# One-hots of a gate crossing: made by VectorE in one operation, multiplied by the gates on ScalarE

## The chip, the cores and the metric

The kernel runs on one core of one Trainium2 chip. The metric is the device time of one execution, in microseconds (us). The core has five engines that run their own instruction lists and meet at semaphores: TensorE (PE; PEld is its weight load), VectorE (DVE), ScalarE (ACT), GpSimd (POOL) and SyncE (SP).

## The reference

Three blocks of layers follow each other over 256 tokens of width 1024: two layers of feed-forward and mixed attention, two layers of feed-forward with a convolution and with stick-breaking attention, and a third block of two attention layers, each followed by a "peer" layer. This case is about the peer layers alone. Each of the 8 heads picks 16 of 128 x 128 experts for a token, so 128 (first key, second key, gate) triples a token:

```python
def peer_ffn(x, w_q, sub_keys, u, v):
    q = (x @ w_q).reshape(B, S, PEER_HEADS, 2, hq)
    s_half = jnp.einsum('bshpc,hpkc->bshpk', q, sub_keys).astype(jnp.float32)
    top_s, top_i = lax.top_k(s_half, PEER_TOPK)
    ...
    gate = jax.nn.softmax(best_s, axis=-1)
    def one_chunk(args):
        xc, ec, gc = args
        h = jax.nn.gelu(jnp.einsum('ted,td->te', u[ec], xc))
        return jnp.einsum('te,ted->td', gc.astype(h.dtype) * h, v[ec])
```

## The kernel before

The kernel gathers no expert. It computes the hidden values of all 16384 experts for all tokens, multiplies them by a dense matrix of gates that is zero where an expert was not picked, and sends all through the second matrix. Weights come in slabs of 1 MB (128 x 2048 floats). SyncE loads them into a ring of 4 (`RING`), ScalarE rounds each into a high part (`round_slab`, L1388, ring of `PARTS` = 3), VectorE subtracts to get the low part (`rest_slab`, L1867), and TensorE multiplies three products for every pair of tiles (L630, L631, L632).

A peer stage has 64 rounds of "up" (two key rows a round, one slab) and 64 of "down". The first 32 rounds of up run while VectorE picks the experts. Then the **crossing** begins, which this change is about: 14 further rounds of up (`EXTRA`), cut into 28 half rounds, with 32 batches of 8 tokens between them (`v.batches`: none in the first two half rounds and none in the last two, and one or two after each of the 24 between, so 2.67 a round). For a batch b:

- VectorE makes `firsts` (L2515, one operation over 8 x 128) and `seconds` (L2518, eight operations, one a token: compare the second key with 0..127 and multiply by the gate in the same instruction). Both have two buffers, so batch b waits until batch b - 2 is crossed.
- TensorE's `cross` (L1367) multiplies, for each token, firsts by seconds: the 128 x 128 matrix of gates of that token, in PSUM.
- VectorE's `multiply` (L2533) applies one half of the gates to hidden values that lie in SBUF. ScalarE's `stage_gates` (L1794) then copies the other half out of PSUM, and `store_gates` (L1801) sends it to DRAM one batch later; it comes back in the second half of the stage.

Each engine's list is in the order of the code. In a round, ScalarE has `round_slab`, then the batches of its first half round, then `activate` (the Gelu of the up round, L1828), then the batches of its second half round. VectorE has `rest_slab`, then the batches. After the crossing, `separate` (L1837 on ScalarE, L2547 on VectorE) makes the hidden values ready for the first round of down on TensorE. ScalarE stood before `separate` in this order: store of the last batch, wait for all stores, `separate(0)`.

Of the kernel before, what the change touches and what calls it, by code (L numbers as in the profile page):

```python
# [160 lines left out]
class Machine:  # L161


    def __init__(self, nc, dram, out, ctx, plan):
# [15 lines left out]
        def signal(name, step=1):  # L180
            self.signals.append(Signal(ctx, nc, name, step))
            return self.signals[-1]
# [78 lines left out]
        self.key_scored, self.key_shown, self.activated = signal("key_scored"), signal("key_shown"), signal("activated")  # L261
        self.gate_shifted, self.gate_powered, self.gate_ready = signal("gate_shifted"), signal("gate_powered"), signal("gate_ready")
        self.slots_turned, self.slotted = signal("slots_turned"), signal("slotted")
        self.hot, self.crossed, self.staged = signal("hot"), signal("crossed"), signal("gates_staged")
        self.gates_stored = [signal(f"gates_stored{i}", 16) for i in range(2)]
        self.gates_back = [signal(f"gates_back{i}", 16) for i in range(RETURNS)]

# [280 lines left out]
def peer_views(k):  # L548
    v = Views()

    v.hidden = k.carve(2 * HALF + 2 * EXTRA, T)
    end = k.taken
    k.taken = 0
    v.early = k.early
    k.taken = DC * 2 * T
    v.h = k.carve(DC, T)
    v.square, v.squares, v.rstd, v.scales = k.carve(DC, T), k.carve(2, T), k.carve(T + TT), k.carve(TT)
    assert k.taken <= 2 * HALF * T
    k.taken = 2 * HALF * T
    v.keys, v.s, v.cand = k.carve(2 * PH, P), k.carve(PH, 4, P), k.carve(2, TT, 256)  # L560
    assert k.taken <= end
    k.taken = end
    v.slots = k.carve(3, T)
    mark = k.taken
    v.hot = k.carve(4 * TOPK, TOPK)
    k.taken = mark
    v.firsts = k.carve(2, BATCH, P)
    v.seconds = [k.carve(BATCH, NKEYS)]
    assert k.taken <= k.room_words - 4 * 2 * T
    k.taken = mark  # L570
    v.returned = k.carve(RETURNS, BATCH, NKEYS // 2)

    k.taken = k.room_words - 4 * 2 * T
    v.seconds.append(k.carve(BATCH, NKEYS))
    v.staged = k.carve(2, BATCH, NKEYS // 2)
    assert k.taken <= k.room_words
    v.crossings = [k.wide_banks[i].rearrange("p (t n) -> p t n", n=NKEYS) for i in (0, 1, 3)]

    k.taken = k.room_words - 4 * 2 * T
    v.chosen, v.q, v.at = k.carve(TT, 3, NSEL), k.carve(2, T), k.carve(2, TT, TOPK, dt=U32)  # L580
    v.best, v.found, v.index = k.carve(2, 4, TOPK), k.carve(2, 4, TOPK, dt=U32), k.carve(2, 4, TOPK)
    v.part, v.ranks, v.small = k.carve(4, TOPK, dt=U32), k.carve(4, TOPK), k.carve(TT, 3, PH)
    v.tops = [v.chosen[:, i, 2, :].rearrange("p (h j) -> p h j", h=PH) for i in range(TT)]

    v.seq = peer_order()
    v.up_at = [v.seq.index(("up", r)) for r in range(ROUNDS)]
    v.down_at = [v.seq.index(("down", r)) for r in range(ROUNDS)]

    late = HALF + EXTRA
    v.place = [2 * r if r < late else 2 * (r - late) for r in range(ROUNDS)]  # L590
    windows = 2 * EXTRA - 4
    v.batches = [range(BATCHES * (s - 2) // windows, BATCHES * (s - 1) // windows) if 2 <= s < 2 + windows else range(0) for s in range(2 * EXTRA)]
    return v
# [16 lines left out]
class TensorE:  # L610
# [733 lines left out]
    def expert_down(self, r, e):  # L1344
        k, nc = self.k, self.k.nc
        if e == 0:
            self.pair = self.take()
            nc.tensor.wait_ge(k.hidden_ready.sem, k.hidden_ready.at(r + 1))
        high, low = self.pair
        at = FIRST_HIDDEN + 2 * (r % 2) + e  # L1350
        for c in range(DC):
            cols = slice(e * D + c * P, e * D + (c + 1) * P)
            mm = self.product(k.banks[c // 2][:, (c % 2) * T:(c % 2 + 1) * T], (high[:, cols], low[:, cols]),
                              (k.hidden[:, at, 0, :], k.hidden[:, at, 1, :]),
                              r == 0 and e == 0 and c % 2 == 0, r == ROUNDS - 1 and e == 1, skip_group_check=True)
        if e == 1:
            mm.then_inc(k.slab_done.up())

    def cross(self, v, b):

        k, nc = self.k, self.k.nc
        bank = v.crossings[b % 3]
        nc.tensor.wait_ge(k.hot.sem, k.hot.at(b + 1))
        if b >= 3:
            nc.tensor.wait_ge(k.staged.sem, k.staged.at(b - 2))
        for t in range(BATCH):
            mm = nc.tensor.matmul(bank[:, t, :], v.firsts[:, b % 2, t, :], v.seconds[b % 2][:, t, :], start=True, stop=True)  # L1367
        mm.then_inc(k.crossed.up())


class ScalarE:
# [362 lines left out]
    def peer(self, v, l):  # L1734
        k, nc = self.k, self.k.nc
        self.stage_enters(True)
        self.early_input(v, k.vec(f"l{l}_ffn_norm", 0, DC), v.early)
        nc.scalar.dma_start(v.keys.rearrange("p c n -> p (c n)"), k.dram[f"keys{l}"]).then_inc(k.small.up(), 16)
        for hd in range(PH):
            self.round_slab()  # L1740
            if hd == 1:
                self.root(v.rstd)
            if hd >= 1:
                self.show_keys(v, hd - 1)
            self.evacuate(hd, v.q, self.projected(hd, 0))
            if hd == 2:
                for c in range(DC):
                    nc.scalar.wait_ge(k.scaled.sem, k.scaled.at(c + 1))
                    nc.scalar.activation(k.h[:, c, 0, :], v.h[:, c, :], ACT.Copy).then_inc(k.h_rounded.up())
        self.show_keys(v, PH - 1)  # L1750
        for r in range(HALF):
            self.round_slab()
            self.activate(v, r)
        for r in range(HALF, HALF + EXTRA):
            self.round_slab()
            if r == HALF:
                for i in range(TT):
                    nc.scalar.wait_ge(k.gate_shifted.sem, k.gate_shifted.at(i + 1))
                    nc.scalar.activation(v.tops[i], v.tops[i], ACT.Exp).then_inc(k.gate_powered.up())
            for b in v.batches[2 * (r - HALF)]:  # L1760
                self.stage_gates(v, b)
            self.activate(v, r)
            if r == HALF:
                for i in range(TT):
                    nc.scalar.wait_ge(k.slots_turned.sem, k.slots_turned.at(i + 1))
                    nc.scalar.activation(v.slots[:, 0:3, i * P:(i + 1) * P], k.banks[6 + i][:, 0:3 * P].rearrange("p (a t) -> p a t", a=3),
                                         ACT.Copy).then_inc(k.slotted.up())
            for b in v.batches[2 * (r - HALF) + 1]:
                self.stage_gates(v, b)
        self.store_gates(v, BATCHES - 1)  # L1770
        for i in range(2):
            nc.scalar.wait_ge(k.gates_stored[i].sem, k.gates_stored[i].at(BATCHES // 2))
        self.separate(v, 0)
        for r in range(ROUNDS):
            if r + 1 < ROUNDS:
                self.separate(v, r + 1)
            self.round_slab()
            if r + HALF + EXTRA < ROUNDS:
                self.round_slab()
                self.activate(v, r + HALF + EXTRA)  # L1780
            if r < RETURN_LEAD:
                self.return_gates(v, r)
            for s in range(2 * (r - HALF + EXTRA), 2 * (r - HALF + EXTRA) + 2):
                for b in v.batches[s] if 0 <= s < 2 * EXTRA else ():
                    if b + RETURN_LEAD < BATCHES:
                        self.return_gates(v, b + RETURN_LEAD)

    def stage_gates(self, v, b):

        k, nc = self.k, self.k.nc  # L1790
# [3 lines left out]
        nc.scalar.activation(v.staged[:, b % 2], v.crossings[b % 3][:, :, NKEYS // 2:NKEYS], ACT.Copy).then_inc(k.staged.up())  # L1794
        if b >= 1:
            self.store_gates(v, b - 1)

    def store_gates(self, v, b):
        k, nc = self.k, self.k.nc
# [44 lines left out]
class VectorE:  # L1844
# [547 lines left out]
    def peer(self, v, l):  # L2392
# [25 lines left out]
        for s in range(2 * EXTRA):  # L2418
            if s % 2 == 0:
                self.rest_slab()  # L2420
            for b in v.batches[s]:
                self.multiply(v, b)
                if b + 2 < BATCHES:
                    self.one_hots(v, b + 2)
        self.separate(v, 0)
        for r in range(HALF - EXTRA):
            self.separate(v, r + 1)
# [80 lines left out]
    def one_hots(self, v, b):  # L2508
# [3 lines left out]
        iota = k.const("iota")  # L2512
        if b >= 2:
            nc.vector.wait_ge(k.crossed.sem, k.crossed.at(b - 1))
        nc.vector.tensor_tensor(v.firsts[:, b % 2], v.slots[:, 0, t0:t0 + BATCH].unsqueeze(2).to_broadcast([P, BATCH, P]),  # L2515
                                iota.unsqueeze(1).to_broadcast([P, BATCH, P]), ALU.is_equal)
        for t in range(BATCH):
            hot = nc.vector.tensor_scalar(v.seconds[b % 2][:, t, :], iota, v.slots[:, 1, t0 + t:t0 + t + 1], v.slots[:, 2, t0 + t:t0 + t + 1],  # L2518
                                          ALU.is_equal, ALU.mult)
        hot.then_inc(k.hot.up())  # L2520

    def multiply(self, v, b):

# [390 lines left out]
```

## Time and profile before

| | us |
|---|---|
| median of 3 runs | 4404.26 (4394.09 to 4410.92) |
| the profiled execution, its time | 4411.53 |
| its span, first to last instruction | 4409.8 |
| busy: PE / DVE / ACT | 4125.4 / 2896.7 / 1968.0 |
| first crossing, first one-hot (2717.14) to first down product (2886.70) | 169.6 |
| second crossing, 3759.30 to 3926.10 | 166.8 |

The mean granted clock of TensorE is 0.968 of its full 2.4 GHz. Busy time of an instruction runs from its start to its end; instructions that follow each other on one engine overlap a little, so the step from one start to the next is shorter than the duration.

### The profile page before, as it was taken

How to read it: one execution, taken by the hardware profiler on the slowest of the kernel's cores; microseconds unless marked ns; L12 is line 12 of the kernel's file. 1: busy time of each engine (PE TensorE's matmuls, PEld its weight loads, DVE VectorE, ACT ScalarE, POOL GpSimd, SP SyncE). 2: the span in 40 equal slices, each digit the busy share in tenths (PEclk: the TensorE clock that was granted, in tenths of full speed). 3: DMA queues.
4: the chain of work that ended last, by engine and by line, in shares of the span. 5: the costliest groups of instructions: out<-in, count | busy, mean ns of one | idle time of the engine just before them, and what ended most of it. 6: DMA issues, size and time to landing. Idle time of an engine off the chain costs nothing.

```text
span 4409.8 us, 70621 instructions
## 1 busy us (share of the span) xinstructions
PE 4125.4 (94%) x29942; PEld 3799.0 (86%) x29942; DVE 2896.7 (66%) x4335; ACT 1968.0 (45%) x2524; POOL 195.9 (4%) x225
## 2 busy tenths in 40 slices
PE   7989999899998999979988999999999999889998
PEld 6878888788786888878887899899998899889998
DVE  6666666566754667547645799944855689964664
ACT  4445454454543545445424543334444544334443
POOL 0011000110000000001002100000000000000000
PEclk9989999899999999989998999999999999999999
DMA  5523545245454454433541354345753345345653
GB/s 198 189 102 134 183 174 188 102 144 189 156 190 137 153 191 172 163 106 125 190 151 75 125 182 164 139 168 188 251 186 140 134 164 183 138 156 188 237 199 143
DMA packets 118602, 716.08 MB, mean 162 GB/s; under 512 B 13952, under 2 KB 19728, under 8 KB 37008
## 3 DMA queue, kind: packets, MB, share of 16 engines
q1 hardware_dynamic: 90864, 660.64, 42.2%
q10 hardware_dynamic: 26400, 43.28, 2.8%
q0 software_dynamic: 1024, 7.64, 0.4%
q8 instruction: 238, 3.90, 0.4%
q14 instruction: 76, 0.62, 0.0%
HBM read 690.38 MB, written 21.13 MB: 161 GB/s over the span
## 4 chain that ended last, share of the span: by engine, by line
PE 75%; DVE 15%; ACT 5%; DMA 2%; issue 2%; POOL 1%; ACTq 1%; POOLq 0%; DVEq 0%; SPq 0%
PE psum L701 21%; PE psum L630 13%; PE psum L632 12%; PE psum L631 12%; PE psum L702 10%; DVE slab_low L1867 4%; DVE room L2518 3%; ACT slab_high L1388 2%; DVE room L2515 1%; PE psum L1048 1%; DVE x L1989 1%; POOL room L2571 1%; DMA peer_gates<-room 1%; DVE room L2539 1%; DVE room L2533 1%
## 5 line engine op out<-in xcount | busy, mean ns | idle before, releaser
L1867 DVE TENSOR_TENSOR slab_low<-slab,slab_high 128x2048 fp32r<-128x2048 f32 x622 | 1430.6, 2301 | 813.3 <-ACT slab_high L1388 810.5
L1388 ACT ACTIVATE slab_high<-slab 128x2048 fp32r<-128x2048 f32 x630 | 1186.8, 1884 | 521.3 <-PE psum L702 263.7
L701 PE MATMUL psum<-h_parts,slab_high 128*128 128x512 f32 x2816 | 999.6, 399 | 43.2 <-DVE h_parts L2176 39.4
L630 PE MATMUL psum<-h_parts,slab_high 128*128 128x256 f32 x2880 | 844.4, 293 | 36.6 <-DVE h_parts L2176 23.5
L631 PE MATMUL psum<-h_parts,slab_high 128*128 128x256 f32 x2880 | 826.8, 287 | 0.0
L632 PE MATMUL psum<-h_parts,slab_low 128*128 128x256 f32 x2880 | 826.2, 287 | 0.0
L702 PE MATMUL psum<-h_parts,slab_low 128*128 128x256 f32 x2816 | 792.0, 281 | 0.0
L630 PE MATMUL psum<-hidden_parts,slab_high 128*128 128x256 f32 x2368 | 671.2, 283 | 28.6 <-DVE hidden_parts L2547 16.1
L701 PEld LDWEIGHTS psum<-h_parts,slab_high 128*128 128x128 f32 x2816 | 533.0, 189 | 176.8 <-issue 32.8
L632 PE MATMUL psum<-hidden_parts,slab_low 128*128 128x256 f32 x2368 | 664.6, 281 | 0.0
L631 PE MATMUL psum<-hidden_parts,slab_high 128*128 128x256 f32 x2368 | 664.3, 281 | 0.0
L630 PEld LDWEIGHTS psum<-h_parts,slab_high 128*128 128x128 f32 x2880 | 565.6, 196 | 53.1 <-issue 37.4
L631 PEld LDWEIGHTS psum<-h_parts,slab_high 128*128 128x128 f32 x2880 | 565.5, 196 | 2.5 <-issue 2.4
L632 PEld LDWEIGHTS psum<-h_parts,slab_low 128*128 128x128 f32 x2880 | 564.2, 196 | 0.0
L702 PEld LDWEIGHTS psum<-h_parts,slab_low 128*128 128x128 f32 x2816 | 536.0, 190 | 0.2
L701 PE MATMUL psum<-hidden_parts,slab_high 128*128 128x512 f32 x1408 | 496.3, 395 | 0.0
L630 PEld LDWEIGHTS psum<-hidden_parts,slab_high 128*128 128x128 f32 x2368 | 447.9, 189 | 38.6 <-issue 33.8
L632 PEld LDWEIGHTS psum<-hidden_parts,slab_low 128*128 128x128 f32 x2368 | 448.7, 189 | 0.0
L631 PEld LDWEIGHTS psum<-hidden_parts,slab_high 128*128 128x128 f32 x2368 | 447.8, 189 | 0.0
L702 PE MATMUL psum<-hidden_parts,slab_low 128*128 128x256 f32 x1408 | 396.4, 282 | 0.0
L701 PEld LDWEIGHTS psum<-hidden_parts,slab_high 128*128 128x128 f32 x1408 | 264.6, 188 | 63.3
L1470 ACT ACTIVATE room<-psum 128x512 f32<-128x512 f32 x176 | 104.8, 596 | 365.0 <-PE psum L702 365.0
(330 smaller groups left out, 4529.4 us busy)
## 6 DMA issues: line engine op xcount, KB each, us to landing
slab<-in_up SPq DMA_DIRECT2D x176, 1024.0 KB, 4.8
slab<-in_keys_up SPq DMA_DIRECT2D x128, 1024.0 KB, 4.8
slab<-in_keys_down SPq DMA_DIRECT2D x128, 1024.0 KB, 4.8
slab<-in_down SPq DMA_DIRECT2D x88, 1024.0 KB, 4.8
slab<-in_w_in SPq DMA_DIRECT2D x16, 1024.0 KB, 4.8
slab<-in_wq SPq DMA_DIRECT2D x16, 1024.0 KB, 4.9
peer_gates<-room ACTq DMA_DIRECT2D x64, 256.0 KB, 2.1
room<-peer_gates ACTq DMA_DIRECT2D x64, 256.0 KB, 4.8
```

The source lines that it names most:

```text
L630: nc.tensor.matmul(out, lhs[0], rhs[0], start=first, stop=False, **options)
L631: nc.tensor.matmul(out, lhs[0], rhs[1], start=False, stop=False, **options)
L632: return nc.tensor.matmul(out, lhs[1], rhs[0], start=False, stop=last, **options)
L701: nc.tensor.matmul(out, lhs[0], rhs, start=first, stop=False, **options)
L702: return nc.tensor.matmul(out[:, 0, :], lhs[1], rhs[:, 0, :], start=False, stop=last, **options)
L1048: mm = nc.tensor.matmul(k.banks[6][:, at:at + P], v.probs[:, n % 5, e, kt * P:(kt + 1) * P], v.diagonals[:, n % 3, e, :], start=True, stop ...
L1388: nc.scalar.activation(k.high[m % PARTS][:, 0:width], k.slabs[m % RING][:, 0:width], ACT.Copy).then_inc(k.rounded.up())
L1470: nc.scalar.activation(v.seconds[:, f % 2], k.bank_pairs[(f + k.first_pair) % 4][:, :, T:2 * T], ACT.Copy).then_inc(k.up_copied.up())
L1867: nc.vector.tensor_tensor(k.low[m % RING][:, 0:width], k.slabs[m % RING][:, 0:width], k.high[m % PARTS][:, 0:width], ALU.subtract).then_in ...
L1989: add = nc.vector.scalar_tensor_tensor(out=both, in0=k.bank_pairs[j][:, :, a * T:(a + 1) * T], scalar=0.5, in1=both, op0=ALU.mult, op1=ALU ...
L2515: nc.vector.tensor_tensor(v.firsts[:, b % 2], v.slots[:, 0, t0:t0 + BATCH].unsqueeze(2).to_broadcast([P, BATCH, P]), iota.unsqueeze(1).to_ ...
L2518: hot = nc.vector.tensor_scalar(v.seconds[b % 2][:, t, :], iota, v.slots[:, 1, t0 + t:t0 + t + 1], v.slots[:, 2, t0 + t:t0 + t + 1], ALU.i ...
```

## The change

VectorE makes `seconds` in one operation over 8 x 128, as it makes `firsts`, without the gate, and makes them first. ScalarE multiplies the gates in (`gate_seconds`): eight activations a batch, in place, the scale a column of `v.slots`. TensorE waits for both. The batch's order on VectorE is turned round (one-hots of b + 2, then the multiply of b). The last store is issued right behind its batch, and `separate(0)` stands ahead of the wait for the stores. The PSUM banks of the crossings go round in another order, and the first down product waits until all gates are copied out.

```diff
-    v.crossings = [k.wide_banks[i].rearrange("p (t n) -> p t n", n=NKEYS) for i in (0, 1, 3)]
+    v.crossings = [k.wide_banks[i].rearrange("p (t n) -> p t n", n=NKEYS) for i in (1, 3, 0)]
...
 class TensorE: def expert_down(self, r, e)
+            if r == 0:
+                nc.tensor.wait_ge(k.staged.sem, k.staged.at(BATCHES))
...
 class TensorE: def cross(self, v, b)
-        nc.tensor.wait_ge(k.hot.sem, k.hot.at(b + 1))
+        nc.tensor.wait_ge(k.firsts_made.sem, k.firsts_made.at(b + 1))
+        nc.tensor.wait_ge(k.seconds_gated.sem, k.seconds_gated.at(b + 1))
...
 class ScalarE: def peer(self, v, l)
             for b in v.batches[2 * (r - HALF)]:
+                self.gate_seconds(v, b + 2)
                 self.stage_gates(v, b)
             self.activate(v, r)
             if r == HALF:
...
+                self.gate_seconds(v, 0)
+                self.gate_seconds(v, 1)
             for b in v.batches[2 * (r - HALF) + 1]:
+                self.gate_seconds(v, b + 2)
                 self.stage_gates(v, b)
-        self.store_gates(v, BATCHES - 1)
+        self.separate(v, 0)
         for i in range(2):
             nc.scalar.wait_ge(k.gates_stored[i].sem, k.gates_stored[i].at(BATCHES // 2))
-        self.separate(v, 0)
...
+    def gate_seconds(self, v, b):
+
+        k, nc = self.k, self.k.nc
+        if b >= BATCHES:
+            return
+        nc.scalar.wait_ge(k.seconds_made.sem, k.seconds_made.at(b + 1))
+        for t in range(BATCH):
+            hot, at = v.seconds[b % 2][:, t, :], b * BATCH + t
+            gated = nc.scalar.activation(hot, hot, ACT.Copy, scale=v.slots[:, 2, at:at + 1])
+        gated.then_inc(k.seconds_gated.up())
...
 class ScalarE: def stage_gates(self, v, b)
+        if b == BATCHES - 1:
+            self.store_gates(v, b)
...
 class VectorE: def peer(self, v, l)
             for b in v.batches[s]:
-                self.multiply(v, b)
                 if b + 2 < BATCHES:
                     self.one_hots(v, b + 2)
+                self.multiply(v, b)
...
 class VectorE: def one_hots(self, v, b)
-        nc.vector.tensor_tensor(v.firsts[:, b % 2], v.slots[:, 0, t0:t0 + BATCH].unsqueeze(2).to_broadcast([P, BATCH, P]),
-                                iota.unsqueeze(1).to_broadcast([P, BATCH, P]), ALU.is_equal)
-        for t in range(BATCH):
-            hot = nc.vector.tensor_scalar(v.seconds[b % 2][:, t, :], iota, v.slots[:, 1, t0 + t:t0 + t + 1], v.slots[:, 2, t0 + t:t0 + t + 1],
-                                          ALU.is_equal, ALU.mult)
-        hot.then_inc(k.hot.up())
+        keys = iota.unsqueeze(1).to_broadcast([P, BATCH, P])
+        for which, dst, made in ((1, v.seconds[b % 2], k.seconds_made), (0, v.firsts[:, b % 2], k.firsts_made)):
+            nc.vector.tensor_tensor(dst, v.slots[:, which, t0:t0 + BATCH].unsqueeze(2).to_broadcast([P, BATCH, P]), keys, ALU.is_equal).then_inc(made.up())
```

The line numbers below are those of each kernel. On ScalarE, at the start of the crossing, before (L1766 copies the keys and gates of the tokens out of PSUM, L1388 rounds a slab, L1794 copies a batch's gates out, L1828 is the Gelu):

```order
L1766 ACTIVATE room<-psum 128x3x128 x2
L1388 ACTIVATE slab_high_58<-slab_50 128x2048
L1794 ACTIVATE room<-psum 128x512
L1828 ACTIVATE room<-psum 128x512
L1794 ACTIVATE room<-psum 128x512
L1801 DMA peer_gates<-room 128x512
L1388 ACTIVATE slab_high_59<-slab_51 128x2048
```

The same place in the changed kernel (L1803 multiplies the gates in; L1771, L1392, L1812, L1848, L1821 are the lines above):

```order
L1771 ACTIVATE room<-psum 128x3x128 x2
L1803 ACTIVATE room<-room 128x128 x16
L1392 ACTIVATE slab_high_58<-slab_50 128x2048
L1803 ACTIVATE room<-room 128x128 x8
L1812 ACTIVATE room<-psum 128x512
L1848 ACTIVATE room<-psum 128x512
L1803 ACTIVATE room<-room 128x128 x8
L1812 ACTIVATE room<-psum 128x512
L1821 DMA peer_gates<-room 128x512
L1392 ACTIVATE slab_high_59<-slab_51 128x2048
L1803 ACTIVATE room<-room 128x128 x8
```

In each round the gating of a batch now stands directly behind the rounding of a slab, and the next rounding stands behind all gatings of the round.

On VectorE, at the same place, before (L1867 makes the low part of a slab, L2533 is the multiply):

```order
L2515 TENSOR_TENSOR room<-room,consts 128x1024
L2518 TENSOR_SCALAR room<-consts,room 128x128 x8
L1867 TENSOR_TENSOR slab_low_53<-slab_49,slab_high_57 128x2048
L1867 TENSOR_TENSOR slab_low_54<-slab_50,slab_high_58 128x2048
L2533 TENSOR_TENSOR room<-psum,room 128x64x8
L2515 TENSOR_TENSOR room<-room,consts 128x1024
L2518 TENSOR_SCALAR room<-consts,room 128x128 x8
```

And in the changed kernel (L2537 are the one-hots, seconds then firsts, L1887 the low part, L2550 the multiply):

```order
L2537 TENSOR_TENSOR room<-room,consts 128x1024 x4
L1887 TENSOR_TENSOR slab_low_53<-slab_49,slab_high_57 128x2048
L1887 TENSOR_TENSOR slab_low_54<-slab_50,slab_high_58 128x2048
L2537 TENSOR_TENSOR room<-room,consts 128x1024 x2
L2550 TENSOR_TENSOR room<-psum,room 128x64x8
L2537 TENSOR_TENSOR room<-room,consts 128x1024 x2
L2550 TENSOR_TENSOR room<-psum,room 128x64x8
L1887 TENSOR_TENSOR slab_low_55<-slab_51,slab_high_59 128x2048
```

The one-hots have moved ahead of the multiply, and a slab's low part still stands ahead of the first one-hots of its round.

## Rows read from the trace of the kernel before

**Rows 1.** waits of PE in the first crossing (line waited for: us in total, times, longest)

```profile
PE psum L1367 <- DVE room L2518: 20.9, 11, 4.0
PE psum L630 <- DVE hidden_parts L2547: 7.4, 1, 7.4
```

**Rows 2.** the same view, second crossing

```profile
PE psum L1367 <- DVE room L2518: 23.1, 14, 2.2
```

**Rows 3.** groups by line, 2712 to 2900 us (busy, mean ns; idle before)

```profile
L1867 DVE TENSOR_TENSOR slab_low<-slab,slab_high 128x2048 fp32r<-128x2048 f32 x16 | 36.6, 2293 | 12.7 <-ACT slab_high L1388 12.7
L1388 ACT ACTIVATE slab_high<-slab 128x2048 fp32r<-128x2048 f32 x16 | 30.5, 1906 | 6.9 <-PE psum L632 6.7
L1794 ACT ACTIVATE room<-psum 128x512 f32<-128x512 f32 x32 | 19.1, 598 | 109.1 <-DVE room L2533 79.4 <-DMA peer_gates<-room 29.7
```

**Rows 4.** timeline of DVE, first crossing (start, duration)

```profile
2717.14 1.23 DVE L2515 TENSOR_TENSOR room<-room,consts 128x1024 f32<-128x1024 f32 x1 [1.49 <-ACT room L1766]
2718.28 2.14 DVE L2518 TENSOR_SCALAR room<-consts,room 128x128 f32<-128x128 f32 x8
2720.33 1.22 DVE L2515 TENSOR_TENSOR room<-room,consts 128x1024 f32<-128x1024 f32 x1
2735.49 2.29 DVE L1867 TENSOR_TENSOR slab_low<-slab,slab_high 128x2048 fp32r<-128x2048 f32 x1
2737.70 0.69 DVE L2533 TENSOR_TENSOR room<-psum,room 128x512 f32<-128x512 f32 x1
2738.30 1.22 DVE L2515 TENSOR_TENSOR room<-room,consts 128x1024 f32<-128x1024 f32 x1
```

**Rows 5.** timeline of PE, a stretch without a wait

```profile
2798.45 1.95 PE L1367 MATMUL psum<-room 128*128 128x128 f32 x16
2800.16 0.36 PE L630 MATMUL psum<-h_parts,slab_high 128*128 128x256 f32 x1
2803.11 1.95 PE L1367 MATMUL psum<-room 128*128 128x128 f32 x16
```

**Rows 6.** timeline of ACT: eight with a scale pointer, two without

```profile
2033.46 3.31 ACT L1446 ACTIVATE h_parts<-x,vectors 128x256 fp32r<-128x256 f32 x8 [3.83 <-PE psum L632]
2036.67 2.18 ACT L1448 ACTIVATE room<-x 128x512 f32<-128x512 f32 x4
...
2713.70 0.51 ACT L1759 ACTIVATE room<-room 128x128 f32<-128x128 f32 x2
```

**Rows 7.** groups of ACT by shape: the exponential with a pointer operand

```profile
L1637 ACT ACTIVATE room<-room 128x256 f32<-128x256 f32 x80 | 40.0, 501 | 62.4 <-DVE room L2207 42.2 <-DVE room L2212 20.2
L1637 ACT ACTIVATE room<-room 128x128 f32<-128x128 f32 x80 | 31.4, 393 | 49.2 <-DVE room L2207 35.7 <-DVE room L2212 13.5
```

**Rows 8.** timeline of ACT, then of PE, end of the first crossing

```profile
2879.34 0.60 ACT L1828 ACTIVATE room<-psum 128x512 f32<-128x512 f32 x1 [3.45 <-PE psum L632]
2879.35 0.35 ACTq L1801 DMA_DIRECT2D peer_gates<-room  x1
2885.20 1.15 ACT L1837 ACTIVATE hidden_parts<-room 128x512 fp32r<-128x512 f32 x2 [5.26 <-DMA peer_gates<-room]
...
2886.70 0.55 PE L630 MATMUL psum<-hidden_parts,slab_high 128*128 128x256 f32 x1 [7.40 <-DVE hidden_parts L2547]
```

**Rows 9.** timeline of DVE, then of PE: start and end, second crossing

```profile
3759.30 1.23 DVE L2515 TENSOR_TENSOR room<-room,consts 128x1024 f32<-128x1024 f32 x1 [1.49 <-ACT room L1766]
...
3926.10 0.55 PE L630 MATMUL psum<-hidden_parts,slab_high 128*128 128x256 f32 x1 [7.43 <-DVE hidden_parts L2547]
```

**Rows 10.** stretches: busy of PE, PEld, DVE, ACT, POOL; granted clock; DMA share; GB/s

```profile
2750.00:2760.00 10.00, 7.81 (x55) 7.62 (x54) 10.00 (x23) 2.14 (x4) 0.00 (x0) 0.83 0.49 157
2880.00:2890.00 10.00, 3.30 (x15) 3.33 (x16) 3.11 (x3) 2.95 (x3) 0.00 (x0) 0.57 0.39 131
```

**Rows 11.** timeline of PE: the crossing after the longest wait

```profile
2868.94 3.79 PE L1367 MATMUL psum<-room 128*128 128x128 f32 x16 [3.97 <-DVE room L2518]
```

**Rows 12.** the stores of the gates, landing

```profile
DMA to landing us min/median/max: 2.0/2.1/5.9
```

More of the change, by code:

```diff
@@ L263, in __init__ @@
         self.slots_turned, self.slotted = signal("slots_turned"), signal("slotted")
-        self.hot, self.crossed, self.staged = signal("hot"), signal("crossed"), signal("gates_staged")
+        self.firsts_made, self.seconds_made, self.seconds_gated = signal("firsts_made"), signal("seconds_made"), signal("seconds_gated")
+        self.crossed, self.staged = signal("crossed"), signal("gates_staged")
         self.gates_stored = [signal(f"gates_stored{i}", 16) for i in range(2)]
```

## Prediction, made before the changed kernel ran

> **What bounds the kernel now.** I read the waits first, since TensorE is busy nearly everywhere and only stretches where it waits can give time back. In the first crossing it waits 20.9 us in 11 pieces for L2518, the gated one-hots, and once 7.4 us at the first down product [rows 1]; in the second, 23.1 us in 14 pieces [rows 2] and 7.43 us [rows 9]. These 58.8 us are what the change aims at. The stretch from 2750 to 2760 us shows VectorE busy all of 10.00 us and TensorE 7.81 [rows 10].
>
> The timeline of VectorE gives its steps, start to start [rows 4]: firsts 1.14 us, eight seconds 2.05, a slab's low part 2.21, a multiply 0.60. A round has 2.67 batches, so VectorE needs 2.21 + 2.67 x 3.79 = 12.3 us. TensorE without a wait takes 1.71 us for a batch and 2.95 for a half round [rows 5]: 2.67 x 1.71 + 2 x 2.95 = 10.5 us. ScalarE has little to do and sits idle 109.1 us before its copies L1794 [rows 3]. So VectorE sets the pace, 1.8 us a round above TensorE.
>
> The 7.4 us at the end come from the last store. It is issued at 2879.35, behind the Gelu that waits for TensorE, and `separate` starts only at 2885.20, after 5.26 us of waiting for that store; TensorE starts at 2886.70 [rows 8].
>
> **VectorE's part.** Seconds become one operation of the same shape as firsts: 1.14 us in place of 2.05, 0.91 less a batch. A round on VectorE falls to 2.21 + 2.67 x 2.88 = 9.9 us. If nothing else happened, TensorE at 10.5 us would be the bound.
>
> **ScalarE's part, the price that the trace doesn't show.** No activation of 128x128 with a scale pointer, SBUF to SBUF, is in the trace. The nearest rows: eight of 128x256 with a scale pointer start at 2033.46 and the next instruction at 2036.67, 0.401 us each [rows 6]. Half the width takes 0.108 us off (501 less 393 ns, an exponential with a pointer operand at both widths [rows 7]), which gives 0.293. I take 0.30 us, 2.40 a batch. Below, the bound is two of 128x128 without a pointer: 0.51 us together, less the last one's overlap of 0.09 (2.14 against 2.05 at L2518), 0.21 each [rows 6, 4]; above, 0.39, the whole duration of rows 7 without any overlap. The Trainium skill (ScalarE: Activation LUTs, What ACT_TABLE_LOAD costs) has 186 ns + 0.833 ns an element, 93 ns for each pointer and 93 ns of overlap, so 293 ns here; by that the sum would be 30 x 8 x 0.007 = 1.7 us less in each crossing.
>
> **The ring that this makes.** The lists show that each engine now waits for the other inside every round. ScalarE's gating of the round's first batch stands right behind `round_slab`. It waits for the seconds, and VectorE makes them only after the low part of that same slab, which waits for `round_slab`. VectorE cannot work ahead: with 2.88 us a batch against ScalarE's 2.89 it has done all it may by then and waits for the rounded slab. So from the start of `round_slab` to the start of the gating pass 1.91 (L1388) + 2.21 + 1.23 + two handovers of about 0.03 = 5.4 us [rows 3, 4], of which ScalarE works 1.9 and stands 3.5. The other steps on ScalarE: 2.40 gating and 0.49 copy a batch, 0.49 Gelu (both last 0.60 us [rows 3, 8], of which I take 0.11 as overlap with the next instruction). A round on ScalarE is thus 5.4 + 0.49 + 2.67 x 2.89 = 13.6 us, above VectorE's old 12.3. The bound moves from VectorE to the ring of the two and gets longer, although each engine alone has less than TensorE's 10.5 or little more.
>
> Queued behind the gating on ScalarE are the copy L1794 of batch b - 2, its store, the Gelu, and the next `round_slab`. TensorE waits for the gating directly, and for the slab through VectorE. A store lands 2.1 us after its issue at the median, 5.9 at most [rows 12]; copies are now 2.89 us apart or more, so most stores have landed, and I add nothing for them. SyncE's loads are issued when TensorE frees a slab; they were early and stay so.
>
> **The sum for the first crossing.** First one-hot at 2717.14 as before. Seconds of batch 1 are ready at 2717.14 + 3 x 1.14 + 0.12 = 2720.7, gated at 2723.1. From there to the gating of batch 31 ScalarE does 12 starts of a round (12 x 5.4 = 64.8), 11 Gelus (5.4), 30 gatings (72.0) and 29 copies (14.2): 2879.5. Then TensorE crosses batch 31 (1.7) and does two half rounds (5.9): 2887.1. The Gelu (0.49), and from `separate` to TensorE 1.50 as between 2885.20 and 2886.70 [rows 8]: 2889.1, where before had 2886.70. That is +2.4. Inside it the new order of the last store earns 5.3 us: the wait of 5.26 is gone from the path.
>
> Second crossing: the same 172.0 us from 3759.30 give 3931.3 against 3926.10 [rows 9], +5.2.
>
> Two terms for the clock. A crossing that starts after a wait of 3.97 us took 3.79 us in place of 1.95 [rows 11, 5]: TensorE had fallen to half its clock. The new waits are about 3.5 us, once a round, so some crossings will be slow. Most of that falls where TensorE has slack (13.6 less 10.5); the part that reaches the ring is that one-hots of b + 2 wait for crossing b. I take 4 us a crossing stage, a third of a round's 1.8 us for some 7 of 12 rounds; 0 if it stays in the slack, 22 (12 x 1.8) if all of it reaches the ring. The other way, the long idle at the end is shorter, 2.3 us in place of 7.4; the stretch 2880 to 2890 has a clock of 0.57 [rows 10], and I take 1 us a stage as saved.
>
> Sum: 2.4 + 5.2 + 2 x 4 - 2 x 1 = +13.6, so 4411.5 + 14 = 4425.5 for an execution like the profiled one. That one is 7.3 us above the median of the runs, so against the median I forecast 4404.3 + 14 = **4418 us**, +0.3%.
>
> The new wait for `staged` at the first down product costs nothing: the last copy stands three short steps (1.5 us) and two waits of at most 2.1 for stores behind the last gating, 5.7 us, and the two half rounds with the crossing take 7.6. If both stores landed at their latest (5.9), it would come some 6 us late. The bank order and the semaphore names cost nothing: they move no work.
>
> **Rivals.**
> - *The gating is cheap* (0.21 us): 30 x 8 x 0.09 = 21.6 us less a stage by the sum, but then copies lie 2.2 us apart and wait for the stores' 2.1, and VectorE's 9.9 and TensorE's 10.5 stay; I allow 10 of it. 4418 - 20 = 4398, no change to be told. The pointer rows speak against it.
> - *No ring* (faster): if ScalarE were far enough ahead that the gating never waited behind a slab, TensorE would be the bound. Waits of 20.9 and 23.1 go, and 5 of each 7.4 at the end: -54 us, 4350. It decides if VectorE's next seconds are done before `round_slab` ends; the lists put the low part between, which speaks against it. A half of it (a ring in some rounds) gives some 4375.
> - *The ring and the slow clock together* (slower): if each round's crossing runs at half the clock and the one-hots wait for it, +22 a stage in place of 4: 4418 + 36 = 4454. It decides from about 1 us a round on. The Trainium skill (ScalarE: Activation LUTs, Rules for kernel authors) says to multiply on VectorE and not on ScalarE. Here one VectorE instruction of 0.26 us a token had the multiply for nothing, and it is now 0.14 on VectorE and 0.30 on ScalarE [rows 4, 6]. By that rule the exchange loses, and it belongs to this case. A gating of 0.33 instead of 0.30 gives +14 and ends on this side too.
>
> **Chances.** Ring as summed 0.52, cheap gating 0.10, no ring or half a ring 0.13, slower than summed 0.25. About 0.5% (22 us) is what a measurement of this kernel tells from no change: faster 0.14, same 0.58, slower 0.28. The range 4382 to 4452 leaves out the whole of "no ring" and the worst of the slow case. The forecast's own range is 4405 to 4435.
>
> **What the profile would show.** Right: L1803 about 390 ns each; some 12 waits a stage of 3 to 4 us on ScalarE before L1803, ended by L2537, and on VectorE before L1887, ended by L1392; TensorE waiting for L1803, above 20.9 us a stage; the wait at the first down product down to 2 or 3 us; from one-hot to first down product 174 to 180 us. Wrong: TensorE with nearly no wait in the crossing, or L1803's step below 0.25 us. A stage over 185 us would be the slower rival.

## The result, and the profile after

| | before | after |
|---|---|---|
| median, us (14 runs each) | 4405.91 | 4424.00 |
| ratio | 1 | 1.0037, 95% interval 1.0028 to 1.0046 |
| span of the profiled execution | 4409.8 | 4425.9 |
| first crossing, first one-hot to first down product | 169.6 | 176.0 |
| second crossing | 166.8 | 173.6 |

The change made the kernel slower by 0.37%: 18 us, where the prediction had 14. Of the 16.1 us between the two profiled executions, 6.4 and 6.8 lie in the two crossings. The other 2.9 come from the rest of the kernel, whose code is the same (the start of the first crossing is 5.8 us later, and 2.9 are won back behind it). In the ten traces used here the first crossing starts anywhere from 2710.6 to 2722.9 us, behind the same code, so a few us outside the crossings say nothing of the change.

The waits of the changed kernel, first crossing (line waited for: us in total, times, longest), which answer to [rows 1] and [rows 3]:

```profile
ACT room L1803 <- DVE room L2537: 46.7, 16, 3.5
DVE slab_low L1887 <- ACT slab_high L1392: 41.4, 14, 3.5
PE psum L1371 <- issue: 27.5, 12, 3.3
PE psum L1371 <- ACT room L1803: 2.3, 2, 1.8
PE psum L631 <- DVE hidden_parts L2564: 2.0, 1, 2.0
```

The same view, second crossing, answering to [rows 2]:

```profile
ACT room L1803 <- DVE room L2537: 46.0, 17, 3.5
PE psum L1371 <- issue: 27.8, 14, 3.3
```

TensorE waits 29.8 us for its crossings in the first one, where it waited 20.9. The profile calls most of it "issue". The crossing waits on two semaphores, and behind such a wait it starts 0.1 us after the gating ends (at 2748.32 behind 2748.22, at 2763.77 behind 2763.68), so I read these as waits for L1803. The wait at the first down product is 2.0 us, where it was 7.4.

One round on ScalarE, the rounding of a slab and the gating behind it (timeline: start, duration):

```profile
2755.83 1.91 ACT L1392 ACTIVATE slab_high<-slab 128x2048 fp32r<-128x2048 f32 x1
2761.23 1.86 ACT L1803 ACTIVATE room<-room 128x128 f32<-128x128 f32 x6 [3.50 <-DVE room L2537]
```

and what VectorE does in between:

```profile
2757.76 2.29 DVE L1887 TENSOR_TENSOR slab_low<-slab,slab_high 128x2048 fp32r<-128x2048 f32 x1 [3.07 <-ACT slab_high L1392]
2759.97 2.35 DVE L2537 TENSOR_TENSOR room<-room,consts 128x1024 f32<-128x1024 f32 x2
2762.24 0.68 DVE L2550 TENSOR_TENSOR room<-psum,room 128x512 f32<-128x512 f32 x1
```

From the start of the rounding to the gating pass 5.40 us, of which ScalarE stands 3.50. The low part starts as the rounding ends (2757.74), the seconds behind it, and the gating as they end. The groups by line, 2712 to 2905 us (busy, mean ns, idle before), against [rows 3]:

```profile
L1803 ACT ACTIVATE room<-room 128x128 f32<-128x128 f32 x256 | 78.1, 390 | 46.8 <-DVE room L2537 46.7
L1812 ACT ACTIVATE room<-psum 128x512 f32<-128x512 f32 x32 | 18.5, 578 | 2.0 <-DVE room L2550 1.6 <-DMA peer_gates<-room 0.4
L1887 DVE TENSOR_TENSOR slab_low<-slab,slab_high 128x2048 fp32r<-128x2048 f32 x16 | 36.7, 2293 | 41.5 <-ACT slab_high L1392 41.4
```

ScalarE's copy L1812 waited 109.1 us before and waits 2.0 now: the gating (78.1 us) and its own waits (46.8) fill that time. VectorE's low part waits 41.5 us for ScalarE, where it was 12.7. Busy time in the two crossings (columns: us, then PE, PEld, DVE, ACT, POOL, granted clock, DMA share, GB/s):

```profile
2722.90:2898.90 176.00, 143.94 (x1131) 141.09 (x1129) 125.52 (x112) 123.83 (x317) 0.00 (x0) 0.94 0.35 127
3770.40:3944.10 173.70, 141.47 (x1131) 138.44 (x1130) 125.44 (x112) 123.89 (x318) 0.00 (x0) 0.96 0.36 128
```

No engine is busy more than 144 of 176 us. ScalarE and VectorE have 124 and 126 each; what fills the rest is that they wait for each other. The stores of the gates now land in 2.0 us, 3.2 at most, against [rows 12]:

```profile
DMA to landing us min/median/max: 2.0/2.0/3.2
```

### The profile page after: what moved, and what is told of

Its sections match the earlier page's. It is cut to its first block, busy times and chain, and to the rows that moved or that the text cites. A ratio compares the mean times of both kernels' runs of the same rounds, so it can differ in the third digit from the quotient of the medians.

```text
span 4425.9 us, 70691 instructions
## 1 busy us (share of the span) xinstructions
PE 4135.4 (93%) x29942; PEld 3805.0 (86%) x29942; DVE 2839.9 (64%) x3887; ACT 2112.6 (48%) x3036; POOL 195.7 (4%) x225
## 4 chain that ended last, share of the span: by engine, by line
PE 75%; DVE 12%; ACT 8%; issue 2%; POOL 1%; DMA 1%; ACTq 1%; POOLq 0%; DVEq 0%; SPq 0%
PE psum L702 20%; PE psum L631 13%; PE psum L633 12%; PE psum L632 12%; PE psum L703 10%; DVE slab_low L1887 4%; ACT slab_high L1392 3%; ACT room L1803 2%; DVE room L2537 1%; DVE x L2009 1%; POOL room L2588 1%; DVE room L2556 1%; PE psum L1049 1%; PE psum L1032 1%; PE psum L1371 1%
## 5 line engine op out<-in xcount | busy, mean ns | idle before, releaser
L1887 DVE TENSOR_TENSOR slab_low<-slab,slab_high 128x2048 fp32r<-128x2048 f32 x622 | 1430.1, 2300 | 885.8 <-ACT slab_high L1392 882.9
L1392 ACT ACTIVATE slab_high<-slab 128x2048 fp32r<-128x2048 f32 x630 | 1186.4, 1883 | 518.1 <-PE psum L703 264.3
```

Of the source, the lines that this page charges most:

```text
L1392: nc.scalar.activation(k.high[m % PARTS][:, 0:width], k.slabs[m % RING][:, 0:width], ACT.Copy).then_inc(k.rounded.up())
L1887: nc.vector.tensor_tensor(k.low[m % RING][:, 0:width], k.slabs[m % RING][:, 0:width], k.high[m % PARTS][:, 0:width], ALU.subtract).then_in ...
```

## The experiments

Two theories stood against each other. **Ring**: the time is lost because ScalarE's gating waits for VectorE's low part of the slab that ScalarE has just rounded. **Work**: the 75 us of gating on ScalarE cost what they cost, in whatever order. Kernels of one group ran on the same chip beside the kernel before.

| experiment | median, us | ratio to before, interval | crossings, us |
|---|---|---|---|
| the changed kernel | 4424.0 | 1.0037 (1.0028 to 1.0046) | 176.0, 173.6 |
| 1 one-hots ahead of the slab | 4378.5 | 0.9935 (0.9917 to 0.9953) | 155.9, 153.7 |
| 2 whole batch ahead of the slab | 4354.9 | 0.9886 (0.9870 to 0.9903) | 142.4, 141.8 |
| 3 store order alone | 4393.9 | 0.9966 (0.9952 to 0.9980) | 164.3, 161.4 |
| 4 no gating | 4394.1 | 0.9974 (0.9959 to 0.9989) | 159.7, 159.7 |
| 5 gating without a pointer | 4399.9 | 0.9977 (0.9965 to 0.9990) | 160.8, 163.3 |
| 6 old store order | 4436.4 | 1.0061 (1.0038 to 1.0084) | 181.0, 180.6 |
| 7 multiply first | 4447.9 | 1.0084 (1.0056 to 1.0112) | 187.9, 188.0 |
| 8 old one-hots, batch ahead | 4388.9 | 0.9955 (0.9936 to 0.9974) | 157.9, 157.5 |

The median of before was 4403.8 in the first four and 4409.9 in the last four. The ratios are taken over all runs, not from the medians, and the two can differ by 0.1%; where a few us matter, the crossings decide; each is read from one trace. The time of the changed kernel, 4424.0, was taken beside runs of before with a median of 4405.9, so differences across groups carry an uncertainty of a few us as well.

### 1. The one-hots of a round's first batch ahead of the slab

```diff
         for s in range(2 * EXTRA):
+            ahead = v.batches[s][0] if s % 2 == 0 and len(v.batches[s]) else BATCHES
+            if ahead + 2 < BATCHES:
+                self.one_hots(v, ahead + 2)
             if s % 2 == 0:
                 self.rest_slab()
             for b in v.batches[s]:
-                if b + 2 < BATCHES:
+                if b != ahead and b + 2 < BATCHES:
                     self.one_hots(v, b + 2)
                 self.multiply(v, b)
```

> The changed kernel, with VectorE making the one-hots of a round's first batch before the slab's low part and not behind it. Ring theory: ScalarE's wait of 3.50 us behind each rounding of a slab, before the gating, goes, 12 times a crossing. What is left of the ring runs through the multiply (low part 2.2, then multiply 0.6, then the copy on ScalarE), so not all comes back: a crossing takes some 20 us less than 176.0 and 173.6, and the median falls from 4424 to about 4382, below the 4406 of the kernel before. Work theory (ScalarE's 2.34 us of gating a batch is itself what costs the time, whatever the order): 4424 stays, within 5. Clock theory (slow crossings make the difference): a few us.

Same instructions, same counts, one place changed in VectorE's list, and 45 us less than the changed kernel. Its waits, first crossing:

```profile
DVE slab_low L1887 <- ACT slab_high L1392: 32.7, 13, 5.8
ACT room L1812 <- DVE room L2553: 10.2, 11, 1.5
ACT room L1803 <- DVE room L2540: 4.0, 7, 1.3
```

ScalarE's wait for one-hots fell from 46.7 us in 16 pieces to 4.0 in 7. The copy L1812 now waits for the multiply in small pieces, the rest of the ring that was foreseen. A crossing is 20 us shorter, as expected. The work theory, by which the order makes no difference, is refuted; that the work costs nothing is not shown by this (experiments 4 and 5 price it).

### 2. The whole first batch ahead of the slab

```diff
-            if s % 2 == 0:
-                self.rest_slab()
-            for b in v.batches[s]:
+            for n, b in enumerate(v.batches[s]):
                 if b + 2 < BATCHES:
                     self.one_hots(v, b + 2)
                 self.multiply(v, b)
+                if s % 2 == 0 and n == 0:
+                    self.rest_slab()
+            if s % 2 == 0 and len(v.batches[s]) == 0:
+                self.rest_slab()
```

> The changed kernel, with the whole first batch of a round (one-hots and multiply) ahead of the slab's low part on VectorE. Ring theory: neither the gating nor the copy of that batch waits for the slab any more; a crossing is about 30 us shorter than the changed kernel's, TensorE's own 10.5 us a round nearly the bound, median about 4364. Work theory: 4424. If the low part comes too late for TensorE instead (a wait of TensorE for L1887's line before its up products), it gives back some of this, and the first experiment is the better one.

69 us less than the changed kernel, and 1.1% faster than the kernel before, the best version of the study. Two roundings on ScalarE and the gating behind each:

```profile
2771.12 1.90 ACT L1392 ACTIVATE slab_high<-slab 128x2048 fp32r<-128x2048 f32 x1
2772.93 0.68 ACT L1803 ACTIVATE room<-room 128x128 f32<-128x128 f32 x2
...
2782.25 1.90 ACT L1392 ACTIVATE slab_high<-slab 128x2048 fp32r<-128x2048 f32 x1
2784.05 1.26 ACT L1803 ACTIVATE room<-room 128x128 f32<-128x128 f32 x4
```

The gating starts 1.80 us behind the start of the rounding, where it took 5.40: here it does not wait at all. Over the first crossing it still waits for one-hots 12.3 us in 12 pieces, 1.8 us at the longest, where it was 46.7. TensorE's waits in the first crossing are nearly gone:

```profile
PE psum L1371 <- issue: 3.8, 6, 1.1
PE psum L631 <- DVE hidden_parts L2566: 4.1, 1, 4.1
```

A crossing is 33.6 and 31.8 us shorter, where some 30 were expected. TensorE is busy 132.8 of the 142.4 us, at a granted clock of 1.00, where it was busy 143.9 of 176.0 at 0.94. So its clock came back with the shorter waits, and the 33.6 us hold that as well; no run separates the two.

### 3. The store order alone

The kernel before, with these edits and the waits for `staged` and the bank order of the change:

```diff
-        self.store_gates(v, BATCHES - 1)
+        self.separate(v, 0)
         for i in range(2):
             nc.scalar.wait_ge(k.gates_stored[i].sem, k.gates_stored[i].at(BATCHES // 2))
-        self.separate(v, 0)
...
         if b >= 1:
             self.store_gates(v, b - 1)
+        if b == BATCHES - 1:
+            self.store_gates(v, b)
```

> The kernel before, with only the other parts of the change: last store issued with its batch, separate(0) ahead of the wait for the stores, the new bank order and the wait at the first down product. By my sum this part earns the wait of 5.26 us at each of the two ends, and a little of the clock: 11 to 13 us, so 4406 becomes about 4394. If that wait was hidden by something else, 4406 stays, and then the one-hots cost less than I reckoned.

9.9 us by the medians (15 by the ratio, 9 to 21); the crossings are 5.3 and 5.5 us shorter, the wait of 5.26 us of [rows 8] once each. The bank order and the wait at the first down product have no run of their own; beside 5.26 us nothing is left for them in the crossings. The waits for one-hots are as in [rows 1]:

```profile
PE psum L1369 <- DVE room L2521: 21.1, 11, 4.0
```

### 4. No gating

```diff
     def gate_seconds(self, v, b):
...
+        return
...
-        nc.tensor.wait_ge(k.seconds_gated.sem, k.seconds_gated.at(b + 1))
+        nc.tensor.wait_ge(k.seconds_made.sem, k.seconds_made.at(b + 1))
```

> The changed kernel without ScalarE's gating: TensorE takes the plain second one-hots, so the gates are left out of the product (each picked expert counts with 1). It shows what the gating costs in all. Ring theory: the ring stays through one-hots, multiply and copy (2.2 + 2.3 + 0.6 us behind each slab on ScalarE), so it does not reach TensorE's bound: about 16 us less a crossing than the changed kernel, 4392. Work theory: with the work gone TensorE is the bound, the 44 us of waits for one-hots go as well as the 10 at the ends, 4350.

With all of the gating gone, a crossing is still 17 to 18 us longer than in the second experiment, which does all of it. So in this order the gating costs 30 us (4424.0 less 4394.1), and the order itself 69 (experiment 2). The ring is there without it, through the multiply:

```profile
2768.38 1.90 ACT L1392 ACTIVATE slab_high<-slab 128x2048 fp32r<-128x2048 f32 x1
2775.52 0.60 ACT L1808 ACTIVATE room<-psum 128x512 f32<-128x512 f32 x1 [5.23 <-DVE room L2546]
```

7.14 us from the rounding to the copy behind it, 5.23 of them waiting.

### 5. Gating with a constant scale

```diff
-            gated = nc.scalar.activation(hot, hot, ACT.Copy, scale=v.slots[:, 2, at:at + 1])
+            gated = nc.scalar.activation(hot, hot, ACT.Copy, scale=1.0)
```

> The changed kernel, its eight gating activations with a constant scale of 1 in place of the pointer to the gate (the gates are left out of the product). It prices the gating: 0.293 us a step in the changed kernel, some 0.21 here by the two activations without a pointer in the trace of before, 0.67 us less a batch and so up to 20 less over a crossing's 30 batches if ScalarE's work counts in full. Ring theory: the waits behind each slab stay (12 of about 3.5 us) and the rest of the loop, with TensorE, takes over before all 20 are back: about 13 us less a crossing than the changed kernel, 4398. Work theory: each us of gating is a us of time, 4424 - 40 = 4384.

Each activation is shorter by about 95 ns (the line's engine, operation, count: ns min, median, max; 388 before):

```profile
L1803 ACT ACTIVATE room<-room x512: 292/293/314, 2719.2 to 3901.9; 128x128 f32<-128x128 f32 x171
```

and the wait behind the slab is the same 3.49:

```profile
2770.81 1.91 ACT L1392 ACTIVATE slab_high<-slab 128x2048 fp32r<-128x2048 f32 x1
2776.21 1.71 ACT L1803 ACTIVATE room<-room 128x128 f32<-128x128 f32 x8 [3.49 <-DVE room L2537]
```

24 us came back by the medians (26 by the ratios), 15.1 and 10.4 in the crossings, against 22.8 a crossing (30 x 8 x 0.095) if ScalarE's work counted in full. The ring theory's 4398 is 2 us off, the work theory's 4384 is 16 (12 by the ratio). This parts the theories less sharply than the first two experiments: gatings are terms of the ring as well, and the 13 us a crossing were an allowance for what else would take over.

### 6. The changed kernel with the old store order

The diff of the third experiment, backwards, on the changed kernel; its bank order and its wait at the first down product stay.

> The changed kernel with the last store and the wait for the stores where they were before. The reordering alone earned 10 us on the kernel before (4404 to 4394). If the two parts add up, this is about 4424 + 10 = 4434 and the one-hot part alone costs 28 against 4406; a crossing is 4 to 5 us longer than 176.0 and 173.6. If the changed kernel's tail hid something else already, 4424.

The last store goes out behind the Gelu again, and `separate` waits for it:

```profile
2887.98 0.35 ACTq L1820 DMA_DIRECT2D peer_gates<-room  x1
2893.77 1.15 ACT L1856 ACTIVATE hidden_parts<-room 128x512 fp32r<-128x512 f32 x2 [5.20 <-DMA peer_gates<-room]
```

4436.4 against 4409.9: without its other part the one-hot part costs 26.5 us. The two parts nearly add up: 26.5 - 9.9 = 16.6, where the whole change measured 18.

### 7. The changed kernel, multiply first

```diff
             for b in v.batches[s]:
+                self.multiply(v, b)
                 if b + 2 < BATCHES:
                     self.one_hots(v, b + 2)
-                self.multiply(v, b)
```

> The changed kernel with VectorE's old order within a batch (multiply of b, then one-hots of b + 2). Ring theory: the multiply of 0.60 us now stands between the slab's low part and the seconds that ScalarE waits for, so the wait behind each slab grows from 3.50 to 4.1 us, and each batch's one-hots come later as well: 7 us a crossing from the first (12 x 0.6), up to 13 with the second, 4438 to 4450. Work theory: the same work, 4424.

```profile
2771.01 1.90 ACT L1392 ACTIVATE slab_high<-slab 128x2048 fp32r<-128x2048 f32 x1
2777.01 0.40 ACT L1803 ACTIVATE room<-room 128x128 f32<-128x128 f32 x1 [4.09 <-DVE room L2537]
```

The wait behind the slab grew from 3.50 to 4.09, the multiply's 0.60. The crossings are 11.9 and 14.4 us longer, where 7 to 13 were expected. The waits behind the slabs make 7 of them (12 x 0.59). For the rest the trace shows the other part that was foreseen, one-hots that come later: the multiply, now first, waits for TensorE's crossing 15.5 us in 8 pieces in the first crossing, with the one-hots behind it, and ScalarE waits for one-hots 60.0 us in all, where it was 46.7. So the turned order of the change was worth 24 us by the medians (21 by the ratios), 26 in the crossings.

### 8. The old one-hots with the batch ahead of the slab

The third experiment's kernel, with the second experiment's edit around the old order of multiply and one-hots.

> The store order of the third experiment with the old gated one-hots on VectorE, and the first batch of a round ahead of the slab's low part, as in the second experiment. It asks whether that experiment's gain is the order's alone. Ring theory: here VectorE has 12.3 us of work in a round and bounds it whatever the order, so only its few waits for ScalarE's slab go: 0 to 6 us under 4394. If the order alone were worth what it gave the changed kernel (69 us), this would come near 4325.

The order is worth 5 us here by the medians (4393.9 against 4388.9) and by the ratios (0.9966 and 0.9955, whose intervals overlap), and 6.4 and 3.9 us in the crossings. VectorE, busy 152.9 of the 157.9 us of the first crossing, still bounds it:

```profile
PE psum L1369 <- DVE room L2523: 16.9, 12, 3.8
PE psum L630 <- DVE hidden_parts L2552: 3.6, 1, 3.6
```

So the order is worth 5 to 10 us where VectorE has the work of the gates, and 69 (65 in the crossings) where ScalarE has it. Within a batch this kernel keeps the multiply first, unlike experiment 2; with 5 us of a crossing left idle on VectorE, turning that round could not be worth more.

## Why the prediction was right

- **The ring.** Right in place and size. 5.4 us from rounding to gating were forecast and 5.40 measured, once a round. Experiments 1 and 2 show that this order is the cause, and 7 that it grows by what is put into it.
- **The price of the gating.** 0.30 us a step was taken. Measured is 0.293 (4.78 us for the first 16, less the last one's 0.39, over 15), mean duration 390 ns. The pointer rows of [rows 6, 7] gave 0.293 exactly; rounding up cost 1.7 us a crossing, which hid a part of the next item.
- **The sum for a crossing.** 172.0 us plus 4 for slow crossings, less 1 behind it: 175 each. Measured 176.0 and 173.6, the second just under the 174 to 180 that the prediction named. The gating of batch 31 ends 164.4 and 163.6 us behind the first one-hot, where 162.4 were summed: less 1.7 for the cheaper gating, plus the 3.5 and 2.8 us of the next item, that sum gives 164.2 and 163.5. From there to the first down product it took 11.5 and 10.0 us in place of 9.6. In the first of them the granted clock was 0.50 from 2889.5 to 2892.0, so the 1 us a stage that was taken as saved there did not show.
- **The clock.** The 4 us a crossing were a guess, of the right size. No run takes the clock alone, but the trace shows what it put on the ring. TensorE waits 3.3 us for a batch eight times in the two crossings. Seven times its `cross` of that batch then lasted 3.04 to 3.75 us, once 2.02 us. Behind a slow `cross`, VectorE's one-hots waited for TensorE, and ScalarE's gating for them:

```profile
2748.32 3.37 PE L1371 MATMUL psum<-room 128*128 128x128 f32 x16 [3.32 <-issue]
2751.73 2.36 DVE L2537 TENSOR_TENSOR room<-room,consts 128x1024 f32<-128x1024 f32 x2 [1.38 <-PE psum L1371]
2752.99 1.87 ACT L1803 ACTIVATE room<-room 128x128 f32<-128x128 f32 x6 [0.94 <-DVE room L2537]
...
2873.15 2.02 PE L1371 MATMUL psum<-room 128*128 128x128 f32 x16 [3.33 <-issue]
```

The granted clock was 0.56 in the first `cross` shown and 1.00 in the last, behind which neither engine waits. ScalarE has three such waits in the first crossing (0.94, 1.22 and 1.32, together 3.5 us) and four in the second (0.61 to 0.81, together 2.8), one behind each slow `cross`. That the clock need not reach a ring shows in experiment 4: granted clocks of 1.00 and 0.95, and 159.7 us both times.
- **What the sum leaves out.** The crossings grew by 13.2 us together, where 13.6 were summed: errors of 1 to 2 us in both directions cancel. The median moved by 18. The prediction has no term for the rest, and none of the experiments explains it; the same code takes several us more or less from trace to trace.
- **The end of the crossing.** Right: the wait of 5.26 us is gone, and experiment 3 measured 5.3 and 5.5 us for it. ScalarE's end of the first crossing in the changed kernel, the last gating, then the Gelu with `separate` directly behind it:

```profile
2885.00 1.86 ACT L1803 ACTIVATE room<-room 128x128 f32<-128x128 f32 x6 [3.50 <-DVE room L2537]
2896.91 0.60 ACT L1848 ACTIVATE room<-psum 128x512 f32<-128x512 f32 x1 [2.83 <-PE psum L633]
2897.40 1.14 ACT L1857 ACTIVATE hidden_parts<-room 128x512 fp32r<-128x512 f32 x2
```

- **The rivals.** "Gating is cheap" was refuted by 0.293 us a step; what it would have been worth shows in experiment 5, 24 us in all, where the text allowed 20. "No ring" was refuted for this kernel, but its 4350 is near what it costs to take the ring away: 4355 in experiment 2. The slower rival did not come: it needed about 1 us in every round, and the clock put 3.5 and 2.8 us on the whole of a crossing.
- **Against the Trainium skill** (ScalarE: Activation LUTs, Rules for kernel authors). Its rule to multiply on VectorE was cited for the slower side. The change was slower, but that rule is not the whole reason: without the gating the changed kernel still takes 4394.1 us, no less than experiment 3 with the gates on VectorE (4393.9). With the slab behind the first batch, the multiply on ScalarE is some 30 us faster than on VectorE (0.9886 against 0.9955, and 15.5 and 15.7 us in the crossings), against the rule, since here VectorE was the bound and ScalarE stood idle.

## What to carry to other kernels

Before moving work to an idle engine, write both engines' lists side by side and look for a wait that crosses back: here ScalarE rounded a slab and then waited for one-hots that VectorE made only after its own work on that slab. Two engines with 124 and 126 us of work took 176 us so, and 142 once the work on the slab stood three instructions later in VectorE's list. Undo the parts of a change one by one as well: here a part that gained 10 us stood beside one that cost 27.

## What the runs showed of the hardware

An activation of 128x128 with a scale pointer lasts 388 ns and one with a constant scale 293, both at the median, so the pointer costs 95 ns. A store of the gates (256 KB) landed 2.0 or 2.1 us after its issue at the median of every kernel here. The longest landing was 3.2 us in the changed kernel, 5.9 in the kernel before and 6.2 in experiment 2; it does not follow the pace, for with the old store order, slower than both (181 us a crossing), it was 5.9, and why is open. In the changed kernel a wait of 3.3 us on TensorE was followed by a `cross` below full clock (granted 0.50 to 0.63) seven times of eight.
